# A decoder step on one core: gate chain moved between query chunks, attention values and last sums regrouped, unused products ahead of waits

## The chip, the core and the metric

The kernel runs on one core of a Trainium2 chip. The metric is device microseconds of one launch. A core has TensorE (PE; PEld is its weight load), VectorE (DVE), ScalarE (ACT), GpSimd (POOL) and a queue engine (SP) that issues most DMAs. The engines run their own instruction streams and meet only at semaphores.

## The reference

One step of a trunk with two layers over 512 prompt tokens and 8 x 4 sample tokens (544 rows of 1024). Layer 0 is retention beside memory attention, layer 1 is forgetting attention beside memory attention. Each ends in an output projection, a layer norm, a two-level router that gives every token two of 32 experts, the experts, and a second layer norm.

```python
h = x @ w_in_a; r, s = retention(q, k, v, s0, log_gamma); tok = head_norm(r) * silu(g)     # layer 0
kvf = x @ w_kv_shared; logf = log_sigmoid(f_logit + b_forget); c = cumsum(logf)            # after layer 0
logits = q @ k * scale + c_q - c_k; p = softmax(causal(logits)); tok = p @ v               # layer 1, 12 heads
mem = softmax(mq @ mem_k * scale) @ mem_v                                                  # both layers, 4 heads
x = layer_norm(ALPHA * x + concat(tok, mem) @ w_o); x = layer_norm(ALPHA * x + moe(x))     # both layers
```

## The kernel before, in words

Everything lies in one function `build`, which writes one instruction stream per engine by hand. The order of work on an engine is the order of its text. A `wait_ge` on a semaphore holds all that stands behind it on that engine. Tokens are five tiles of rows (four of 128, one of 32). PSUM has eight banks of 128 x 512, and each stage names its banks.

- **Split products** (`split_product`, lines 706 to 708): projections are done as three products of rounded and remainder parts. Weights come in chunks through two ring buffers: SP loads a chunk (L402) when the chunk two earlier has been used, ACT rounds it (`round_chunk`, L1389), DVE forms the remainder (`split_chunk`, L1823).
- **Gating** (L1134): 30 transposes turn the gated retention rows; PE waits for DVE's scaling (L2156).
- **Memory attention** (`mem_prompt_attention`): for each of four row tiles PE makes logits (L737), DVE takes the maximum (L1763), ACT the exponentials (L1428), DVE scales the rows (L1777), PE turns them (L749), ACT and DVE copy them, PE multiplies by the values (L761). Between these, ACT rounds the eight slices of the output weights (L1400) and DVE forms their remainders. `mem_sample_attention` then turns the cached keys of eight sequences (L783, copied by ACT at L1454), makes their logits (L795), turns the exponentials (L802) and multiplies (L810).
- **Projection and routing** (`project_and_route`, lines 855 to 889): tile by tile PE projects (`project_tile`, two halves of 512 columns), DVE adds the residual (L1860) and normalises (`norm_tile`, lines 1842 to 1850), PE turns the rows (`cols_of`, L700), ACT copies them (`copy_cols`, L1364) and PE makes the router's logits (`router_tile`, L827). Tile i is projected, and directly after it tile i-1 is turned and routed. ACT copies tile i-1 only after it has taken the deviation of tile i (L1369). After the last tile come the slots for experts (L851 to L888) and the gather of the first rows (POOL, L571).
- **Experts** (`experts`, `pair`): 16 pairs; up-products L907, hidden transposes L915, down-products L924. SP streams the weights (L449, L454) as buffers come free. The first pair's buffers are loaded when the last projection is done, the second pair's after the last router tile.
- **Between the layers**: `next_mem_kv` (turning L975, products L1000, both on PE) stands beside `combine(0)` on DVE. Then 20 tiles of keys and values (`token_major`), the 12 gate columns (`gate_columns`, from a chunk of their own), the turning of the keys (L1190), and eight query products (`feature_major`, chunks of `w_in_b`). After the eighth, ACT takes the exponential and the logarithm of the gates (L1662, L1664), and PE makes the running sums (L1207 to L1217).
- **Forgetting attention, prompt**: a pipeline over 12 heads. `minus_c` (L1228) spreads -c over 128 rows by four products; `fox_logits` (L1239); DVE adds and masks (L2199 to L2207); ACT takes the exponentials; `fox_turn` (L1251) makes ten transposes; `fox_values` (L1261) makes ten products with 128 x 128 probabilities as the weights and 64 columns of V moving; DVE scales into `o_rows` (L2213), which 24 transposes turn at the end (L1319).
- **Forgetting attention, samples**: 16 cached pages are turned (L1284) and multiplied (L1307); exponentials L1705; turning L1325; values L1334 and L1339.
- **The end** (`combine(1)`): SP loads the two expert rows of each token two tiles ahead (L497); DVE scales and adds them (L2042, L2043), normalises, and SP stores the tile (L563, L565).

Of the kernel before, what the change touches and what calls it, by code (L numbers as in the profile page):

```python
# [127 lines left out]
def build(nc, x_prompt, x_sample, mem_prompt, state_ret, cache_fox_k, cache_fox_v, cache_fox_logf, cache_mem_k,  # L128
# [12 lines left out]
    with ctx:  # L141
# [98 lines left out]
        eps_ln, eps_hn = sm(1), sm(1)  # L240
        wslot = sm(PAIRS + MORE)
# [25 lines left out]
        chunks.append((cols(w_kv_shared, 1536, 1548), ("tm_mm", 41)))  # L267
# [3 lines left out]
        CH_A, CH_S, CH_B, CH_END = 0, 9, 14, 17  # L271
# [5 lines left out]
        def w_lo(m):  # L277
            return w_raw(m, ring_r)
# [33 lines left out]
        yg = [view(work, 0, 2, D), view(big, 0, 2, D)]  # L312
        RB = 0
# [43 lines left out]
        gate_cols = view(work, 3072, TOK)  # L357

# [4 lines left out]
        PT_AT = {3: 0, 2: 4 * P, 0: 7 * P, 1: 8 * P}  # L363
        LOGIT_AT = {1: (0, 0), 0: (1, 0), 2: (1, P), 3: (2, 0)}
        o_rows = view(x_cols_t, 0, ST, FW)
# [12 lines left out]
        own_row = view(ln_t, (PG * DB + 1) * QR, DB, QR)  # L378
        fkT = [view(work, 3072, 6, P), view(work, 3840, 6, P)]
# [11 lines left out]
        def _(sp):  # L391
# [98 lines left out]
            def expert_rows(l, i):  # L490
                if i == 0:
                    sp.wait_ge(S("y_out"), 16 * PAIRS * (l + 1))
                    sp.wait_ge(S("rows_done"), l + 1)
                if i >= 2:
                    sp.wait_ge(S("yg_used"), NT * l + i - 1)
                n = ROWS[i]
                sp.dma_start(yg[i % 2][0:n], ys.rearrange("(j t) d -> t j d", j=2)[P * i:P * i + n]) \  # L497
                    .then_inc(S(f"yg_in{i % 2}"), 16)
# [58 lines left out]
            for i in range(2):  # L557
                expert_rows(1, i)
            for i in range(2, NT):
                expert_rows(1, i)  # L560
# [8 lines left out]
        def _(pool):  # L569
# [8 lines left out]
            def dispatch(l):  # L578
# [4 lines left out]
                nc.gpsimd.memset(xg, 0.0).then_inc(S("xg_zero"), 1)  # L583
                pool.wait_ge(S("slots"), 3 * l + 1)
                pool.wait_ge(S("xs_out"), 80 * (l + 1))
                pool.wait_ge(S("xg_zero"), l + 1)
# [29 lines left out]
            def mem_outputs(l):  # L616
                pool.wait_ge(S("mkv_ev"), (4, 6)[l])
                for out, lo in ((mem_k_p, 0), (mem_v_p, MW)):
                    pool.dma_start(out[l, 0].rearrange("(t p) h d -> p t (h d)", p=P), memkv[:, l, :, lo:lo + MW]) \
                        .then_inc(S("mp_out"), 16)  # L620
# [24 lines left out]
            pool.dma_start(fox_f_p[0].rearrange("(t p) h -> p t h", p=P), logf[:, 0:ST]).then_inc(S("f_out"), 16)  # L645
            pool.dma_start(fox_f_s.rearrange("b t h -> (b t) h"), logf[0:NS, ST]).then_inc(S("f_out"), 16)
# [5 lines left out]
            pool.wait_ge(S("pool_zero"), 2)  # L652
# [22 lines left out]
            pool.wait_ge(S("f_out"), 32)  # L675
            pool.wait_ge(S("kv_out"), 64)
            pool.wait_ge(S("mp_out"), 64)
# [6 lines left out]
        def _(pe):  # L684
            mm, tr = nc.tensor.matmul, nc.tensor.transpose

# [40 lines left out]
            def mem_prompt_attention(l):  # L727
# [13 lines left out]
                def turn(i):  # L741
                    pe.wait_ge(S("mp_n"), n0 + i + 1)
# [30 lines left out]
            def mem_sample_attention(l):  # L773
# [24 lines left out]
                pe.wait_ge(S("ms_e"), l + 1)  # L798
# [4 lines left out]
                last.then_inc(S("ms_t"), 1)  # L803
                pe.wait_ge(S("ms_c"), l + 1)
# [8 lines left out]
                last.then_inc(S("ms_o"), 1)  # L813

            def mem_sample_columns(l):
                pe.wait_ge(S("ms_n"), l + 1)
                for g in range(2):
                    last = tr(bank(2, P * g, P * g + P), mres[:, g].rearrange("p r d -> p (r d)"), ident)
                last.then_inc(S("ms_r"), 1)
# [11 lines left out]
            def project_tile(l, i):  # L831
# [3 lines left out]
                for half in range(2):  # L835
# [19 lines left out]
            def project_and_route(l):  # L855
# [7 lines left out]
                for i in range(NT + 1):  # L863
                    if 1 <= i < NT:
                        project_tile(l, i)
                    if i == NT - 1:
                        pe.wait_ge(S("onehot"), 2 * l + 1)
                        ranks = rank_bank(l)
                        mm(ranks[:, 0:3], C("strict"), cnt[:, 0:3], start=True, stop=False)
                        mm(ranks[:, 1:3], C("ones"), cnt[:, 0:2], start=False, stop=False)  # L870
                        mm(ranks[:, 2:3], C("ones"), cnt[:, 0:1], start=False, stop=True).then_inc(S("rank_mm"), 1)
# [57 lines left out]
            def experts(l):  # L929
# [4 lines left out]
                pe.wait_ge(S("slots"), 3 * l + 1)  # L934
                pe.wait_ge(S("xg_in"), 16 * (s + 1))
# [57 lines left out]
            def next_mem_kv():  # L993
                pe.wait_ge(S("mem_in"), 64)
# [131 lines left out]
            pe.wait_ge(S("rkd"), 2 * ST + RH)  # L1126
            for i in range(NT):
# [19 lines left out]
            def gate_columns():  # L1147

                chunk_split(pe, 13)
                pe.wait_ge(S("tm_ev"), 38)  # L1150
                w_hi, w_rest = w_r(13), w_lo(13)
                for o, t in ((bank(4, FM0, rows=(0, FH)), slice(0, TOK // 2)),
                             (bank(5, 0, TOK // 2, rows=(0, FH)), slice(TOK // 2, TOK))):
                    for k in range(KD):
                        last = split_product(o, w_hi[:, k, :], w_rest[:, k, :], XT_r[:, k, t], XT_lo[:, k, t], k)
# [37 lines left out]
            pe.wait_ge(S("tk_cp"), NT + NT)  # L1193
            for n in range(2, 10):
                m = CH_B + (n - 2) // 3
                if (n - 2) % 3 == 0:
                    chunk_split(pe, m)
# [4 lines left out]
            pe.wait_ge(S("f_step"), 5)  # L1202
            pe.wait_ge(S("tm_ev"), 42)
            pe.wait_ge(S("pf_in"), 16 * DB * PG)
            for i in range(ST):
                for q in range(i + 1):
# [1076 lines left out]
```

## Time and profile before

| | |
|---|---|
| runs | 1586.42, 1588.14, 1590.35 us, median 1588.14 |
| profiled execution | 1593.53 us, its span 1591.6 us |
| busy | PE 1294.4 us, PEld 890.6, DVE 505.0, ACT 357.4, POOL 101.3 |
| DMA | 316.29 MB, mean 199 GB/s, 420 GB/s in the expert stages |
| mean granted TensorE clock | 0.892 |
| stages, from the chain of waits | layer 0 to the experts 0 to 448 us, experts 448 to 703, keys and queries to 926, prompt heads to 1021, sample pages to 1111, memory and projection to 1284, experts to 1535, end |

The page gives each engine's busy share in 40 equal slices, the TensorE clock that was granted in each (1.00 is 2.4 GHz, 0.50 is 1.2 GHz), and the chain of work that ended last. PE matmul records of float32 products come in twos, so a count of records is twice the count of products there.

### The profile page before, as it was taken

To read this page: it belongs to the slowest core of one execution; us is meant where nothing else is said; L and a number is where in the kernel's file an instruction comes from. 1 tells how busy PE (TensorE), PEld (TensorE's weight loads), DVE (VectorE), ACT (ScalarE), POOL (GpSimd) and SP (SyncE) were. 2 spreads that over 40 slices of the span, in tenths; PEclk is the share of its full clock that TensorE was granted. 3 is DMA by queue.
4 is the path that set the end of the run, shared out by engine and by line. 5 is a ranking of instruction groups with operands and counts; after the bars stand their busy time and mean duration, and the time that the engine had idled before them with its cause. 6 is when DMAs were issued, how large, how long until landed. Compare 5 with 4: busy or idle time off the path is not lost.

```text
span 1591.6 us, 17891 instructions
## 1 busy us (share of the span) xinstructions
PE 1294.4 (81%) x7095; PEld 890.6 (56%) x7095; DVE 505.0 (32%) x1059; ACT 357.4 (22%) x721; POOL 101.3 (6%) x131
## 2 busy tenths in 40 slices
PE   7999987598798777668897899998598799877750
PEld 6999985466543232235796878783466543232220
DVE  3551176533620000008301057314534620000017
ACT  3112232420111111113212236311520111111110
POOL 0000001000011111102000020000000011111100
PEclk9999998797789999988898969798797789999985
DMA  7222117300589999955114140131600589999953
GB/s 284 93 80 80 54 50 237 97 14 27 212 360 420 421 419 420 420 211 203 40 42 164 44 144 1 32 125 46 201 14 27 206 358 420 420 419 420 420 193 111
DMA packets 101991, 316.29 MB, mean 199 GB/s; under 512 B 23058, under 2 KB 55970, under 8 KB 77090
## 3 DMA queue, kind: packets, MB, share of 16 engines
q1 hardware_dynamic: 88978, 284.98, 46.4%
q0 software_dynamic: 12944, 30.36, 5.1%
q8 instruction: 47, 0.77, 0.2%
q14 instruction: 22, 0.18, 0.0%
HBM read 299.61 MB, written 31.42 MB: 208 GB/s over the span
## 4 chain that ended last, share of the span: by engine, by line
PE 58%; DMA 25%; DVE 10%; ACT 4%; issue 1%; SPq 1%; ACTq 0%; POOLq 0%; DVEq 0%
DMA weight_ring<-in_w_up_dram 16%; PE ps L706 9%; PE ps L708 9%; PE ps L707 9%; PE ps L907 6%; DMA mix_cols<-in_w_down_dram 5%; PE ps L924 3%; PE ps L1239 2%; PE ps L1261 2%; PE ps L827 2%; PE ps L1307 2%; DVE small L1842 1%; PE ps L795 1%; DMA work<-stream_rows,ints 1%; PE ps L1000 1%
## 5 line engine op out<-in xcount | busy, mean ns | idle before, releaser
L907 PE MATMUL ps<-expert_weights,work 128*64 128x512 f32 x512 | 128.7, 651 | 39.5 <-DMA expert_weights<-in_w_up_dram 37.0
L2019 DVE TENSOR_TENSOR work<-ps,work 128x256 f32<-128x256 f32 x32 | 13.6, 425 | 439.4 <-ACT work L1494 439.4
L907 PE MATMUL ps<-weight_ring,work 128*64 128x512 f32 x512 | 119.3, 611 | 36.3 <-DMA weight_ring<-in_w_up_dram 36.3
L907 PEld LDWEIGHTS ps<-expert_weights,work 128*64 128x64 f32 x512 | 39.4, 148 | 126.7 <-issue 73.3
L707 PE MATMUL ps<-weight_ring_r,mix_cols_r 128*128 128x384 f32 (+1 forms) x320 | 110.1, 344 | 0.0
L708 PE MATMUL ps<-mix_cols_r,weight_ring_r 128*128 128x272 f32 (+1 forms) x368 | 106.1, 288 | 0.0
L907 PEld LDWEIGHTS ps<-weight_ring,work 128*64 128x64 f32 x512 | 39.7, 139 | 114.9 <-issue 80.5
L1494 ACT ACTIVATE work<-ps 128x256 f32<-128x256 f32 x32 | 12.3, 383 | 277.7 <-PE ps L907 277.7
L924 PE MATMUL ps<-mix_cols,work 128*64 128x512 f32 x256 | 60.2, 611 | 11.5 <-DVE work L2021 6.7
L706 PE MATMUL ps<-expert_weights_r 128*128 128x512 f32 (+1 forms) x160 | 69.1, 432 | 0.0
L708 PEld LDWEIGHTS ps<-mix_cols_r,weight_ring_r 128*128 128x128 f32 (+1 forms) x368 | 67.8, 184 | 0.5
L1504 ACT ACTIVATE work<-ps,small 128x512 f32<-128x512 f32 x64 | 40.5, 683 | 122.7 <-PE ps L924 119.1
L707 PE MATMUL ps<-weight_ring_r,expert_weights_r 128*128 128x512 f32 (+1 forms) x160 | 67.8, 424 | 0.0
L708 PE MATMUL ps<-expert_weights_r,mix_cols_r 128*128 128x512 f32 (+1 forms) x160 | 67.4, 421 | 0.0
L924 PE MATMUL ps<-expert_weights,work 128*64 128x512 f32 x256 | 58.5, 597 | 10.5 <-DVE work L2021 7.9
L706 PE MATMUL ps<-weight_ring_r,mix_cols_r 128*128 128x384 f32 (+1 forms) x160 | 56.7, 354 | 6.1 <-DVE x_cols_r L1815 5.2
L707 PEld LDWEIGHTS ps<-weight_ring_r,mix_cols_r 128*128 128x128 f32 (+1 forms) x320 | 56.6, 177 | 4.3
L706 PE MATMUL ps<-mix_cols_r,weight_ring_r 128*128 128x272 f32 (+1 forms) x192 | 55.7, 290 | 1.6 <-DVE weight_ring_r L1823 1.6
L708 PE MATMUL ps<-weight_ring_r,x_cols_r 128*128 128x384 f32 (+1 forms) x160 | 56.1, 351 | 0.0
L707 PE MATMUL ps<-x_cols_r,weight_ring_r 128*128 128x272 f32 (+1 forms) x192 | 55.2, 288 | 0.0
L1823 DVE TENSOR_TENSOR weight_ring_r<-weight_ring,weight_ring_r 128x1536 fp32r<-128x1536 f32 (+2 forms) x18 | 26.7, 1523 | 83.7 <-ACT weight_ring_r L1389 83.7
L706 PE MATMUL ps<-mix_cols_r,work_r 128*128 128x272 f32 x176 | 51.1, 290 | 0.2 <-ACT expert_weights L1650 0.2
(403 smaller groups left out, 2373.7 us busy)
## 6 DMA issues: line engine op xcount, KB each, us to landing
expert_weights<-in_w_up_dram SPq DMA_DIRECT2D x64, 1024.0 KB, 19.6
weight_ring<-in_w_up_dram SPq DMA_DIRECT2D x64, 1024.0 KB, 20.1
expert_weights<-in_w_down_dram SPq DMA_DIRECT2D x32, 1024.0 KB, 21.9
mix_cols<-in_w_down_dram SPq DMA_DIRECT2D x32, 1024.0 KB, 23.1
weight_ring<-in_w_in_a_dram SPq DMA_DIRECT2D x8, 1536.0 KB, 6.5
weight_ring<-in_w_o_dram SPq DMA_DIRECT2D x4, 2048.0 KB, 13.3
weight_ring<-in_w_kv_shared_dram SPq DMA_DIRECT2D x4, 1536.0 KB, 8.0
weight_ring<-in_cache_fox_k_dram SPq DMA_DIRECT2D x12, 384.0 KB, 4.4
```

The source lines that it names most:

```text
L706: mm(o, a_r, b_r, start=(k == 0), stop=False)
L707: mm(o, a_r, b_lo, start=False, stop=False)
L708: return mm(o, a_lo, b_r, start=False, stop=(k == KD - 1))
L795: last = mm(bank(b // 4, 0, ML, rows=rr), qmb[:, a, 16 * b:16 * b + 32], mkcT[:, b % 2, a, :], start=(a == 0), stop=(a == 1), skip_group_c ...
L827: last = mm(bank(2 + j % 2, 0, NG + NE, rows=(0, n)), XT[:, k, P * i:P * i + n], wr[:, k, :], start=(k == 0), stop=(k == KD - 1))
L907: last = mm(bank(0, rows=(t.start, t.stop)), xgT[:, k, t], WU[2 * q + j][:, k, :], start=(k == 0), stop=(k == KD - 1))
L924: last = mm(bank(4 + half, rows=(t.start, t.stop)), hid_cols[:, f, t], WD[2 * q + j][:, f, 512 * half:512 * half + 512], start=(f == 0), s ...
L1239: last = mm(bank(b, o, o + P * (i + 1)), qT[f, h // 2, P * i:P * i + P], kT[f, h // 2, 0:P * (i + 1)], start=True, stop=True)
L1261: last = mm(bank(7, FD * i, FD * i + FD), fprT[:, h % 2, o:o + P], V[:, q, FD * h:FD * h + FD], start=(q == 0), stop=(q == i))
L1307: last = mm(o, qbd[:, h, b, :], fkT[n % 2][:, h, :], start=False, stop=False, skip_group_check=True)
L1504: last = af(yb[:, 512 * half:512 * half + 512], bank(4 + half), ACT.Copy, scale=wslot[:, i:i + 1])
L1823: v.tensor_tensor(w_lo(m)[:, k, :], w_raw(m)[:, k, :], w_r(m)[:, k, :], ALU.subtract) \
```

## The change

Parts, lettered as the prediction names them. **Unused products**: `keep_clock(b, n)` issues n products of 128 x 512 into a bank that nobody reads; it stands ahead of waits in six places. **Router order**: `project_tile` takes halves, and the router of tile i-2 stands between the halves of tile i; the rank products move behind the last projection. **Gates**: the 12 gate columns leave the chunk ring and get a load of their own; the query chunks therefore come one place earlier. The gate chain on ACT and DVE stands between query chunks and the running sums before query product 8. **Heads**: -c is turned once (`turn_c`) and spread by one product a head; values go by pairs of heads with V as weights, already turned; the reciprocals of the sums are taken once and spread by `row_sums`. **Banks** of the sample stage move from 4-7 to 0-3 and back. **End**: all five row tiles are loaded at once, PE adds the two rows, DVE adds that to the stream, ACT takes sums and squares. Several semaphores are merged under one name.

```diff
+            def keep_clock(b, n):
+                lo = CONST["decay"][0]
+                for _ in range(n):
+                    mm(bank(b), ident, const_t[:, lo:lo + 512], start=True, stop=True)
...
                 def turn(i):
+                    keep_clock(7, 3)
                     pe.wait_ge(S("mp_n"), n0 + i + 1)
...
+                    if b == 0:
+                        keep_clock(7, 4)
                     pe.wait_ge(S("mk_cp"), n0 + b + 1)
...
-                pe.wait_ge(S("ms_e"), l + 1)
+                keep_clock(7, 2)
+                pe.wait_ge(S("ms_step"), 8 * l + 2)
...
                 pe.wait_ge(S("slots"), 3 * l + 1)
+                keep_clock(1, 3)
                 pe.wait_ge(S("xg_in"), 16 * (s + 1))
...
             def next_mem_kv():
+                keep_clock(1, 5)
                 pe.wait_ge(S("mem_in"), 64)
...
+            keep_clock(0, 6)
             for i in range(NT):
                 n = ROWS[i]
                 pe.wait_ge(S("gated"), i + 1)
...
-                for i in range(NT + 1):
-                    if 1 <= i < NT:
-                        project_tile(l, i)
-                    if i == NT - 1:
-                        pe.wait_ge(S("onehot"), 2 * l + 1)
-                        ranks = rank_bank(l)
...
-                    if i:
-                        cols_of(2 * l + 1, i - 1)
-                        router_tile(l, i - 1)
+                project_tile(l, 1)
+                cols_of(2 * l + 1, 0)
+                for i in range(2, NT):
+                    project_tile(l, i, (0,))
+                    router_tile(l, i - 2)
+                    project_tile(l, i, (1,))
+                    cols_of(2 * l + 1, i - 1)
+                pe.wait_ge(S("onehot"), 2 * l + 1)
+                ranks = rank_bank(l)
...
+                router_tile(l, NT - 2)
+                cols_of(2 * l + 1, NT - 1)
+                router_tile(l, NT - 1)
...
-        chunks.append((cols(w_kv_shared, 1536, 1548), ("tm_mm", 41)))
...
+            sp.wait_ge(S("mt_mm"), 8)
+            sp.dma_start(gate_w, cols(w_kv_shared, 1536, 1548)).then_inc(S("gate_w"), 16)
...
+                if j == 34:
+                    act.wait_ge(S("gate_w"), 16)
+                    af(gate_r, gate_w, ACT.Copy).then_inc(S("gate_w"), 1)
-                if j in (22, 26, 31, 36):
+                if j in (22, 26, 31, 37):
                     round_chunk(CH_S + 1 + (j - 20) // 5)
...
-            round_chunk(CH_B)
...
             for n in range(2, 10):
                 m = CH_B + (n - 2) // 3
+                if n == 8:
+                    gate_sums()
...
+                if n == 3:
+                    act.wait_ge(S("f_step"), 1)
+                    af(fe, fe, ACT.Exp, scale=-1.0).then_inc(S("f_step"), 1)
+                if n == 4:
+                    act.wait_ge(S("f_step"), 3)
+                    af(fe, fe, ACT.Ln).then_inc(S("f_step"), 1)
...
-                for q in range(ST):
-                    last = mm(bank(3, P * q, P * q + P), negc[:, q, h:h + 1].broadcast_to([P, P]), ident,
-                              start=True, stop=True)
-                last.then_inc(S("fnb"), 1)
+                mm(bank(3), ident[0:FH, h:h + 1].broadcast_to([FH, P]), negc_cols[0:FH], start=True, stop=True) \
+                    .then_inc(S("fnb"), 1)
...
+                for q in range(ST):
+                    i0 = max(q, 1)
+                    for r in range(2):
+                        rows = (64 * r, 64 * r + 64)
+                        v_q = V[:, q, FD * (2 * p + r):FD * (2 * p + r) + FD]
+                        if q == ST - 1:
+                            moving = fprT[:, r, 9 * P:10 * P]
+                        else:
+                            moving = fprT[:, r, 0:9 * P].rearrange("p (i t) -> p i t", i=3)[:, i0 - 1:, P * q:P * q + P]
+                        last = mm(bank(7, P * i0, SEQ, rows=rows), v_q, moving, start=(q == 0), stop=(q == ST - 1),
+                                  skip_group_check=True)
...
+            for p in range(FH // 2):
+                row_sums(p)
...
+            for i in range(NT):
+                n = ROWS[i]
+                pe.wait_ge(S(f"yl_in{i}"), 16)
+                for half in range(2):
+                    b = 2 * (i % 2) + half
+                    if i >= 2:
+                        pe.wait_ge(S("yg_ev"), 2 * (i - 2) + half + 1)
+                    for j in range(2):
+                        last = mm(bank(b, rows=(0, n)), ident[0:n, 0:n], yg1[i][0:n, j, 512 * half:512 * half + 512],
+                                  start=(j == 0), stop=(j == 1))
+                    last.then_inc(S("yg_sum"), 1)
...
+            def sums_and_deviation(i):
+                n = ROWS[i]
+                act.wait_ge(S("yg_ev"), 2 * i + 2)
+                af(squares[0:n], X[0:n, i], ACT.Copy, accum_out=row_sum[0:n, i:i + 1]).then_inc(S("ln_sq"), 1)
...
+                af(squares[0:n], X[0:n, i], ACT.Square, bias=less_mean[0:n, i:i + 1],
+                   accum_out=row_sq[0:n, i:i + 1]).then_inc(S("ln_sq"), 1)
...
+                af(rstd[0:n, i:i + 1], row_sq[0:n, i:i + 1], ACT.Sqrt, bias=eps_ln[0:n, 0:1], scale=1.0 / D) \
+                    .then_inc(S("ln_sd"), 1)
```

## Rows read from the trace of the kernel before

**Rows 1.** The page: the span, and the granted clock in 40 slices.
```profile
span 1591.6 us, 17891 instructions
...
PEclk9999998797789999988898969798797789999985
```

**Rows 2.** The chain of waits, experts of layer 0: start us, us, what.
```profile
447.61 9.22 PE ps L907 x32
...
475.11 6.87 PE ps L907 x32
...
496.31 28.23 DMA weight_ring<-in_w_up_dram
```

**Rows 3.** What PE waited for, whole span: us in total, times, longest us.
```profile
PE ps L827 <- ACT x_cols L1364: 25.7, 10, 4.5
PE ps L749 <- DVE work L1777: 23.4, 8, 4.1
...
PE ps L1134 <- DVE work L2156: 6.5, 1, 6.5
```

**Rows 4.** Busy by stretch: us, PE, PEld, DVE, ACT, POOL, clock, DMA share, GB/s.
```profile
281.00:306.00 25.00, 16.05 (x96) 12.90 (x96) 9.63 (x15) 9.28 (x28) 0.00 (x0) 0.66 0.46 116
313.00:333.00 20.00, 17.26 (x88) 8.27 (x92) 4.85 (x8) 7.54 (x14) 0.00 (x0) 0.77 0.00 1
...
944.00:1007.00 63.00, 63.00 (x439) 52.13 (x437) 48.55 (x115) 38.41 (x111) 0.00 (x0) 1.00 0.00 1
1008.00:1029.00 21.00, 19.09 (x93) 17.05 (x94) 1.78 (x5) 4.61 (x13) 0.00 (x0) 0.51 0.12 38
1029.00:1082.00 53.00, 50.42 (x448) 41.11 (x445) 7.48 (x16) 12.87 (x25) 0.00 (x0) 1.00 0.40 125
```

**Rows 5.** The chain of waits, queries and prompt heads.
```profile
841.93 12.73 DMA weight_ring<-in_w_in_b_dram
...
926.37 4.56 PE ps L1239 x8
...
947.61 2.35 PE ps L1239 x8
...
951.20 2.18 PE ps L1261 x20
...
957.92 2.18 PE ps L1261 x20
```

**Rows 6.** PE in order of time: start us, us, what, wait and releaser; memory attention.
```profile
281.56 1.97 PE L749 MATMUL ps<-const,work 128*128 128x128 f32 x8 [4.10 <-DVE work L1777]
...
313.01 1.91 PE L795 MATMUL ps<-work,mem_queries 128*32 128x256 f32 x4 [4.20 <-ACT work L1454]
...
333.38 0.50 PE L706 MATMUL ps<-expert_weights_r 128*128 128x512 f32 x1
```

**Rows 7.** DVE in order of time: the residual's last half, first and last tile.
```profile
344.81 0.69 DVE L1860 SCALAR_TENSOR_TENSOR x_rows<-x_rows,ps 128x512 f32<-128x512 f32 x1 [4.88 <-PE ps L708]
...
417.24 0.68 DVE L1860 SCALAR_TENSOR_TENSOR x_rows<-x_rows,ps 32x512 f32<-32x512 f32 x1 [4.81 <-PE ps L708]
```

**Rows 8.** PE in order of time, turning and routing of one tile.
```profile
398.74 1.04 PE L700 MATMUL ps<-const,x_rows 128*128 128x128 f32 x8
402.54 2.19 PE L827 MATMUL ps<-weight_ring,x_cols 128*128 128x36 f32 x16 [2.77 <-ACT x_cols L1364]
```

**Rows 9.** PE in order of time, keys' turning and gate sums.
```profile
858.38 3.45 PE L1190 MATMUL ps<-const,work 128*128 128x128 f32 x18 [9.19 <-ACT expert_weights L1650]
...
915.39 4.45 PE L1207 MATMUL ps<-small,const 128*128 128x12 f32 x20 [4.62 <-DVE small L2179]
```

**Rows 10.** All engines in order of time, the end.
```profile
1547.05 1.23 DVE L2042 SCALAR_TENSOR_TENSOR x_rows<-x_rows,work 128x1024 f32<-128x1024 f32 x1 [7.52 <-DMA work<-expert_rows]
...
1581.08 0.34 SPq L565 DMA_DIRECT2D out_dram<-x_rows  x1
```

**Rows 11.** Groups by line: ACT's table loads ahead of the square roots.
```profile
L1369 ACT ACT_TABLE_LOAD x4 | 5.1, 1283 | 4.8 <-DMA expert_rows<-work,ints 4.7
```

More of the change, by code:

```diff
@@ L312, in build @@
         yg = [view(work, 0, 2, D), view(big, 0, 2, D)]
+        yg1 = [view(big, 2 * D * i, 2, D) for i in range(NT)]
+        squares = view(work, 0, D)
         RB = 0
@@ L357, in build @@
         gate_cols = view(work, 3072, TOK)
+        gate_w, gate_lo = view(work, 3616, KD, FH), view(work_r, 3616, KD, FH)
+        gate_r = view(work_r, 3712, KD, FH)
         fpr = [view(work, 4 * SEQ * k, ST, SEQ) for k in range(2)]
@@ L829, in router_tile, with project_tile @@
                 last.then_inc(S("rt_mm"), 1)
-            def project_tile(l, i):
+            def project_tile(l, i, halves=(0, 1)):
                 n = ROWS[i]
                 pe.wait_ge(S("mix_lo"), NT * l + i + 1)
-                for half in range(2):
+                for half in halves:
                     j = 10 * l + 2 * i + half
@@ L1268, in _, with row_sums @@
                     fox_logits(s)
+                if s % 2 and s >= 3:
+                    fox_values(s // 2 - 1)
                 if 1 <= s <= FH:
                     fox_turn(s - 1)
-                if s >= 2:
-                    fox_values(s - 2)
                 if s + 1 < FH:
                     minus_c(s + 1)
-            pe.wait_ge(S("fp_ev"), FH)
+            pe.wait_ge(S("fp_ev"), FH // 2)
+            pe.wait_ge(S("fp_r"), 1)
+            for i in range(ST):
+                last = tr(bank(3, P * i, P * i + P, rows=(0, FH)), esum_f[:, i, :], ident)
+            last.then_inc(S("fp_r"), 1)
+            def row_sums(p):
+                if p >= 4:
+                    pe.wait_ge(S("tk_cp"), 2 * NT + p - 3)
+                for r in range(2):
+                    last = mm(bank(4 + p % 4, rows=(64 * r, 64 * r + 64)),
+                              ident[0:FH, 2 * p + r:2 * p + r + 1].broadcast_to([FH, FD]), rsum_cols[0:FH], start=True,
+                              stop=True)
+                last.then_inc(S("tk_mm"), 1)
             def turn_page(n):
@@ L1673, in _ @@
             act.wait_ge(S("kv_out"), 64)
+            act.wait_ge(S("fnb"), 1)
+            af(negc_cols[0:FH], bank(7, rows=(0, FH)), ACT.Copy).then_inc(S("fnb_cp"), 1)
             keys_sum(0)
@@ L1686, in _ @@
                     if n == 0 and h >= 2:
-                        act.wait_ge(S("fox_p"), h - 1)
-                    w = 4 * P if n < 2 else 2 * P
-                    af(fprT[:, h % 2, 4 * P * n:4 * P * n + w], bank(4 + n, 0, w), ACT.Copy).then_inc(S("fp_c"), 1)
+                        act.wait_ge(S("fox_p"), h // 2)
+                    lo, hi = PC_AT[n]
+                    af(fprT[:, h % 2, lo:hi], bank(4 + n, 0, hi - lo), ACT.Copy).then_inc(S("fp_c"), 1)
                 if h + 2 < FH:
                     keys_sum(h + 2)
+            act.wait_ge(S("fp_r"), 2)
+            af(rsum_cols[0:FH], bank(3, rows=(0, FH)), ACT.Copy).then_inc(S("fp_r"), 1)
             for n in range(DB * PG):
@@ L1727, in _ @@
             experts(1)
-            norm_and_columns(3, columns=False)
+            for i in range(NT):
+                sums_and_deviation(i)
         @block.vector
```

270 lines of the change are left out of this document (144 added, 126 removed).

## The prediction

> **What bounds the kernel now.** I read the page first [rows 1]: the chain of work that ended last is PE's in most stages, the experts apart, and the granted clock has gaps outside them. The chain of waits then gives the stages: from 496 us on, the experts of layer 0 wait for one load of weights after another [rows 2]. Those loads are released by the first pair's products and by the last projections, so whatever comes earlier ahead of them moves the whole stage earlier, one for one. The list of PE's waits names three that the change aims at: the router for its copied columns 25.7 us, the turning of memory probabilities 23.4, the gating 6.5 [rows 3]. The busy time by stretch shows what such waits cost besides their length: in the memory attention the clock is 0.66 and 0.77, at the end of the heads 0.51, and in the run of heads and of pages 1.00 [rows 4]. The same eight logit products take 4.56 us where the clock is 0.50 and 2.35 where it is 1.00, 1.94 times [rows 5]. So the gain can come from three things: shorter idle time, PE's own work at the higher level (2.4 in place of 1.2 GHz), and less work.
>
> **One unused product.** The up-products of a pair are 32 records of 512 columns, two side by side in 64-wide halves: 6.87 us at full clock, 0.43 a record, and 9.22 while the clock is coming back [rows 2]. A float32 product leaves two records, so one unused product is 0.86 us at full clock and 0.86 x 1.94 = 1.66 at half. Three stand in front of a wait of 23.4/8 = 2.9 on average [rows 3]: 2.6 fit at full clock, 5.0 at half do not. Four stand in front of the first keys' copy, 3.4 against 4.20 [rows 6]; six before the gating, 5.1 against 6.5 [rows 3]. At full clock all of them hide; at half clock they push the stage out.
>
> **The sum**, in us of the profiled execution, each term with its two ends:
>
> Gating: the transposes behind the wait run at the higher level, but DVE's scaling paces most of them: -2 (0 to -3).
>
> Memory attention, prompt, each layer: 16.05 us of PE work at a clock of 0.66 would be 16.05 x 0.66 = 10.6 at 1.00, so -5.5 if the waits between stay [rows 4]. Next to end last would be ACT's rounding of the output weights, done between the same steps. Ends 0 and -9. Samples: 17.26 x (1 - 0.77) = -4.0 (0 to -6). Two layers: -11 and -8.
>
> Router order, each layer. From the first projection at 333.4 [rows 6] the residual of tile 0 starts at 344.8 and that of tile 4 at 417.2 [rows 7]. A tile's projection is 11.2 us (333.4 to 344.6, the tile of 32 rows too, since 512 columns move in every one). Turning takes 1.04 and routing 2.19, and between them PE waits 2.77 for ACT [rows 8]. In the new order the router of tile i-2 has half a projection, 5.6 us, between its turning and itself, twice the wait. PE then does 5 x 11.2 + 3 x 2.2 + 3 x 1.05 + 0.2 = 66, and the last projection ends at 399.4 where it ended at 417.2 less 0.8. I take -17 (the choice of experts on DVE now stands before the last residual; ends -10 and -18), twice: -34. The experts' loads wait for that projection and move with it.
>
> Products before the gather and before the next memory rows: three and five, 5.0 and 8.3 us if they start at half clock. Against that, the first pair's products would go from 9.22 towards 6.87 [rows 2], twice, and DVE's combining covers the second. I take 0 for all of it (-6 to +8).
>
> Keys and queries. Today the chunk of query weights is loaded last (12.73 us on the chain, landing at 854.7 [rows 5]) and the keys' turning waits 9.19 for its rounding [rows 9]. One chunk fewer in the ring puts it a place earlier: -9.6. After the queries PE waits 4.62 for the gate chain on ACT and DVE, then does the sums, of which the first group is 4.45 at half clock [rows 9]; the first logits start at 926.4 [rows 5], 15.6 us behind the last query product (915.39 - 4.62 = 910.8). The chain now runs beside queries 3 to 6, the sums cost 4.1 at full clock ahead of query 8, and about 2.8 are left for turning and spreading -c: -9. Together -18.6 (-12 to -20).
>
> Heads. One head's period is 957.92 - 951.20 = 6.72, of which the values are 2.18 [rows 5]. Two heads' values are now 2,560 columns in two halves at 0.43 per 512, that is 2.15 for both: a pair takes 13.45 - 2.2 = 11.25, six pairs -13.2. The clock before the loop no longer falls, so the first two heads lose their doubled products (2.2 for the logits of each, about 1 for each spreading): -6. Together -19 (-10 to -23). DVE comes next: 48.55 busy of 63 [rows 4], 5.2 a head of which about 0.4 goes, under PE's 5.6.
>
> Sample pages: 24 transposes and their copies become six spreads, and the stretch at 0.51 [rows 4] would be shorter by up to half of its 19.1: -6 (-2 to -9).
>
> The end. Five tiles take DVE 6.8 each, 1547.05 to 1581.08 [rows 10]. New: two adds of 0.69 [rows 7] and two passes of 1.23 [rows 10] with small ones, 4.2; ACT takes two passes, by DVE's row about 3.3 with its small ones. That is -13, but the first tile has to go through PE (four products, 3.4 or 6.6) and ACT, which is some 8 late: -5. If PE stays at half clock, 5 x 6.6 = 33 alone ends it: -9 to +8.
>
> Sum: -2 - 11 - 8 - 34 + 0 - 18.6 - 19 - 6 - 5 = -103.6. The profiled execution took 1593.5, 5.4 above the median, so the change is set against the median: 1588.1 - 103.6 = **1484.5**.
>
> **A rule against the sum.** Long runs made of turns and products together hold 1.00 here (1029 to 1082 [rows 4]). The Trainium skill ("TensorE: Matmul & The Clock Gate", Part 4: PE-mode transpose) says that the full clock does not engage for transposes, as they do not count as busy work in the same way. By it the two memory terms, mostly turns, would give half, and the sum would be about -94; the row stands against it.
>
> **The rivals.** First, the order does less than it says: ACT's copies stay late, so that a layer's router wins only 10, and DVE's chain of maximum and mask holds the heads at 6.72. For it: DVE's 48.55 of 63. Against it: 2.77 of wait against 5.6 of cover. 14 and 13 are lost: 1484.5 + 27 = 1511.5.
>
> Second, the unused products run at half clock and overrun: eight times 5.0 - 2.9, twice 6.6 - 4.2, the gating 3.5, the two ahead of the sample's turning and those before the gather some 6, about 31 in all; and the 21 of gating and memory attention do not come: 1536. For it: the clock is 0.66 where the first of them stand [rows 4]. Against it: they are themselves work without gaps.
>
> Third, Square is not in the table set that Sqrt needs: two loads of 1.283 [rows 11] a tile bring ACT to 5.9 against DVE's 4.2, 10 in all: 1494.5. The Trainium skill ("ScalarE: Activation LUTs", "Table sets: the hidden batching unit") names relu, copy, identity and abs as in every set, and not Square, so it leaves this open; no row shows it.
>
> Fourth, the other side: PE's clock does not hold in the new heads and pages. Heads that are paired let PE pause in every second step, and at half clock the loop's 67.5 become 131 and the pages' 50.4 become 98 [rows 4]: +111, which gives 1595, slower by 7. It decides if the whole stretch from 905 on is at 0.50. For it: 19.09 of 21 us busy at 0.51. Against it: 1.00 from 944 to 1007, and fewer pauses ahead of the loop.
>
> **How the numbers follow.** Forecast 0.57, first rival 0.20, second 0.08, third 0.10, fourth 0.05. 0.3%, about what a measurement can tell from no change, is 4.8 us. Only the fourth, full in force (0.03), is slower; a milder one (0.01) lies within; all else is faster, 0.96. Low end: all the better ends of the terms together are 25 lower, 1460. High end: the first rival with 10 on top, 1522; left out are the second, the fourth and some of the tails.
>
> **What would show it.** Right: PE's wait at the router is gone and the last projection ends 17 earlier; the clock in the memory attention is over 0.9; no wait for the query chunk before the keys; a head every 5.6 us; the last stage 28 us long with a tile each 4.2. Wrong: unused products that still run when their wait has ended, a clock near 0.5 in the heads, table loads beside the square roots of the end, or DVE's idle time gone in the heads with a period over 6.

## The result, and the profile after

| | before | after |
|---|---|---|
| median of the runs | 1587.28 us | 1503.74 us |
| lowest, highest | 1583.45, 1590.35 | 1501.96, 1505.48 |
| profiled execution, its span | 1593.53, 1591.6 | 1503.13, 1501.2 |
| mean granted clock | 0.892 | 0.933 |

The changed kernel is faster: ratio 0.9475, interval 0.945 to 0.9499, that is 83.5 us. The forecast was 1484.5, with a range of 1460 to 1522. The two profiled executions lie 90.4 apart; that of before was itself about 6 above its median.

The page of the kernel after, to be read against [rows 1]:

```profile
span 1501.2 us, 17781 instructions
...
PEclk9999998999799999998899968999999699999987
```

Three slices of the clock stand out now: the one where the experts' slots are made (the 11th), one near 880 us (the 24th, a 6), and the second slot stage (the 32nd). The one near 880 is where the heads begin; the kernel before has a 6 in the same place, so this stretch got nothing back.

What PE waited for, in us in total, times and the longest:

```profile
PE ps L1405 <- DMA expert_weights<-expert_rows: 7.1, 1, 7.1
...
PE ps L844 <- ACT x_cols L1419: 5.8, 4, 2.5
...
PE ps L763 <- DVE work L1847: 1.8, 2, 1.3
```

The router's wait went from 25.7 to 5.8 and the memory turning's from 23.4 to 1.8 [rows 3]; the gating's 6.5 has left the list. L1405 is new: PE adds the rows of the end.

Busy time by stretch (PE, PEld, DVE, ACT, POOL, then clock, DMA share, GB/s), first the memory attention, then the heads' start and run:

```profile
278.00:301.00 23.00, 20.58 (x120) 11.74 (x120) 12.83 (x21) 12.65 (x42) 0.00 (x0) 1.00 0.68 196
301.00:322.00 21.00, 19.36 (x96) 9.64 (x96) 10.02 (x11) 12.09 (x21) 0.00 (x0) 1.00 0.01 1
...
878.00:910.00 32.00, 32.00 (x76) 15.59 (x76) 18.91 (x40) 13.24 (x35) 6.62 (x17) 0.53 0.56 195
910.00:955.00 45.00, 45.00 (x232) 25.44 (x230) 36.01 (x78) 32.64 (x93) 0.00 (x0) 0.99 0.00 1
```

The memory attention runs at 1.00 where it had 0.66 and 0.77 [rows 4]. In the heads PE is busy for all of 878 to 910 and has half its clock.

The chain of waits, from the first spread of -c on (L1252 spread, L1262 logits, L1274 turning, L1294 values):

```profile
877.50 1.09 PE ps L1252 x2
878.59 3.53 PE ps L1262 x8
882.12 2.00 PE ps L1252 x2
884.11 4.56 PE ps L1262 x8
888.67 2.32 PE ps L1274 x10
891.00 2.00 PE ps L1252 x2
893.00 4.56 PE ps L1262 x8
...
907.08 3.62 PE ps L1294 x16
910.70 1.24 PE ps L1274 x10
911.94 1.05 PE ps L1252 x2
912.99 2.35 PE ps L1262 x8
```

The same eight records of logits take 4.56 until 906 and 2.35 from 913 on. PE had been idle for 1.34 us ahead of 877.5; the clock fell 2 us behind that, with PE busy.

Setting the two chains side by side gives what each part moved (start of the same work, before and after; the last column is the change since the line above):

| up to the start of | before | after | moved | this part |
|---|---|---|---|---|
| last retention products | 258.5 | 257.2 | -1.3 | no part of the change |
| first memory exponentials (gating) | 278.1 | 278.6 | +0.5 | +1.8 |
| first projection (memory attention) | 333.4 | 324.5 | -8.9 | -9.4 |
| second slot products (router order) | 432.8 | 403.8 | -29.0 | -20.1 |
| fourth pair of experts | 487.7 | 459.3 | -28.4 | +0.6 |
| first chunk of keys | 761.7 | 729.9 | -31.8 | -3.4 |
| first logits (gates, queries) | 926.4 | 878.6 | -47.8 | -16.0 |
| first page turned (heads) | 1021.1 | 968.0 | -53.1 | -5.3 |
| last values of the pages | 1102.0 | 1044.3 | -57.7 | -4.6 |
| slot products of layer 1 (memory, router) | 1269.1 | 1182.5 | -86.6 | -28.9 |
| first rows of the end | 1547.0 | 1462.0 | -85.0 | +1.6 |
| last store | 1581.1 | 1490.7 | -90.3 | -5.3 |

One line is far from its forecast: the heads, -5.3 for -19. The gain of the router order shows in the chain as full speed: routing a tile takes 1.71 (2.19 in [rows 8]), turning one 0.87, and by the two chains the last residual starts 63.8 us behind the first projection, where it started 83.8 behind it.

```profile
353.68 1.71 PE ps L844 x16
...
388.30 1.28 DVE x_rows L1930 x2
```

### The profile page after: what moved, and what is told of

Same layout as the page of the kernel before. It is cut to its first block, busy times and chain, and to the rows that moved or that the text cites. A ratio compares the mean times of both kernels' runs of the same rounds, so it can differ in the third digit from the quotient of the medians.

```text
span 1501.2 us, 17781 instructions
## 1 busy us (share of the span) xinstructions
PE 1308.6 (87%) x7057; PEld 851.5 (57%) x7057; DVE 492.9 (33%) x1032; ACT 369.0 (25%) x743; POOL 102.0 (7%) x131
## 4 chain that ended last, share of the span: by engine, by line
PE 59%; DMA 25%; DVE 10%; ACT 4%; issue 1%; SPq 1%; POOLq 0%; DVEq 0%; ACTq 0%
DMA weight_ring<-in_w_up_dram 16%; PE ps L719 9%; PE ps L721 9%; PE ps L720 9%; PE ps L927 6%; DMA mix_cols<-in_w_down_dram 6%; PE ps L944 3%; PE ps L1262 2%; PE ps L698 2%; PE ps L1356 2%; PE ps L1252 1%; PE ps L811 1%; PE ps L1274 1%; PE ps L1294 1%; PE ps L1333 1%
## 5 line engine op out<-in xcount | busy, mean ns | idle before, releaser
L927 PE MATMUL ps<-expert_weights,work 128*64 128x512 f32 x512 | 124.4, 633 | 38.3 <-DMA expert_weights<-in_w_up_dram 35.6
L927 PE MATMUL ps<-weight_ring,work 128*64 128x512 f32 x512 | 122.7, 625 | 34.9 <-DMA weight_ring<-in_w_up_dram 34.9
L721 PE MATMUL ps<-mix_cols_r,weight_ring_r 128*128 128x272 f32 x352 | 102.4, 291 | 0.0
L944 PE MATMUL ps<-mix_cols,work 128*64 128x512 f32 x256 | 60.2, 611 | 11.1 <-DVE work L2091 7.3
L944 PE MATMUL ps<-expert_weights,work 128*64 128x512 f32 x256 | 58.5, 597 | 11.3 <-DVE work L2091 6.7
L721 PEld LDWEIGHTS ps<-mix_cols_r,weight_ring_r 128*128 128x128 f32 x352 | 67.2, 191 | 0.0
L719 PE MATMUL ps<-expert_weights_r 128*128 128x512 f32 (+1 forms) x160 | 64.1, 401 | 0.9 <-DVE mix_cols_r L1904 0.9
L719 PE MATMUL ps<-mix_cols_r,weight_ring_r 128*128 128x272 f32 x208 | 61.5, 296 | 1.8 <-DVE weight_ring_r L1893 1.7
L720 PE MATMUL ps<-weight_ring_r,expert_weights_r 128*128 128x512 f32 (+1 forms) x160 | 63.1, 394 | 0.0
L721 PE MATMUL ps<-expert_weights_r,mix_cols_r 128*128 128x512 f32 (+1 forms) x160 | 63.0, 394 | 0.0
L720 PE MATMUL ps<-x_cols_r,weight_ring_r 128*128 128x272 f32 x208 | 60.8, 292 | 0.0
L698 PE MATMUL ps<-const 128*128 128x512 f32 x106 | 58.4, 697 | 1.0 <-DVE ints L2096 1.0
L1893 DVE TENSOR_TENSOR weight_ring_r<-weight_ring,weight_ring_r 128x1536 fp32r<-128x1536 f32 (+1 forms) x18 | 28.7, 1637 | 74.5 <-ACT weight_ring_r L1444 74.5
```

The lines of the kernel that those rows point to most:

```text
L698: mm(bank(b), ident, const_t[:, lo:lo + 512], start=True, stop=True)
L719: mm(o, a_r, b_r, start=(k == 0), stop=False)
L720: mm(o, a_r, b_lo, start=False, stop=False)
L721: return mm(o, a_lo, b_r, start=False, stop=(k == KD - 1))
L927: last = mm(bank(0, rows=(t.start, t.stop)), xgT[:, k, t], WU[2 * q + j][:, k, :], start=(k == 0), stop=(k == KD - 1))
L944: last = mm(bank(4 + half, rows=(t.start, t.stop)), hid_cols[:, f, t], WD[2 * q + j][:, f, 512 * half:512 * half + 512], start=(f == 0), s ...
```

## The experiments

Medians of four runs (six for the last three kernels), each beside runs of the kernel before on the same chip. The chips differ between groups of runs, and the medians of the kernel before lie between 1584.4 and 1590.9 there, so a difference of a few us between two groups tells nothing. Every edit is against the changed kernel unless another is named. The line numbers of these kernels are a few higher than those above.

### A spread of -c over all rows

```diff
-                mm(bank(3), ident[0:FH, h:h + 1].broadcast_to([FH, P]), negc_cols[0:FH], start=True, stop=True)
+                mm(bank(3), ident[:, h:h + 1].broadcast_to([P, P]), negc_cols, start=True, stop=True)
...
+            nc.gpsimd.memset(negc_cols, 0.0).then_inc(S("pool_zero"), 1)
```

> The changed kernel with -c spread by 128 rows of contraction (116 of them zero) in place of 12; the number of columns stays 512 a head. Theory (the heads' missing gain is a clock that stays at 0.50 from 879 to 910 us because the stretch from the last query to the first values is done by thin products, 12-row spreads and 64-row logits): with full rows the clock comes back behind the first turn, as it did in the kernel before, near 892 instead of 910; three steps at half clock become about one and a half, 8 to 12 us are won, about 1493. Rival (the pause of 1.3 us ahead of the first spread lets the clock fall and only time or dense work brings it back, the spread's rows are no matter): unchanged, 1502 to 1506, clock back near 910.

Measured: 1490.99 (ratio 0.9381, 0.9325 to 0.9437), 12.8 below the changed kernel, and 13.2 below the kernel with the pause filled, two sections on, which ran on the same chip. The spread moves as many columns as before. Busy time by stretch of this kernel:

```profile
882.00:886.00 4.00, 4.00 (x12) 1.59 (x11) 3.90 (x8) 1.88 (x2) 3.38 (x12) 1.00 0.99 323
886.00:890.00 4.00, 2.66 (x12) 1.98 (x12) 3.90 (x11) 3.48 (x11) 1.33 (x3) 0.80 1.00 341
890.00:894.00 4.00, 4.00 (x11) 1.56 (x10) 2.11 (x6) 2.74 (x9) 0.00 (x0) 0.77 0.97 342
894.00:898.00 4.00, 4.00 (x20) 2.52 (x20) 3.90 (x10) 2.71 (x7) 0.00 (x0) 1.00 0.96 347
```

The first logits run at full clock, and the dip, behind a wait of 1.3 us, is some 4 us long (0.61 and 0.54 between 888 and 892). The number came out near the theory's 1493. Not all of it is clock. In the run of the loop, where both kernels have 1.00, the spread of 128 rows takes 0.86 in the chain and the one of 12 rows 1.05, so that a pair of heads takes 11.22 (902.85 to 914.07) in place of 11.60 (912.99 to 924.59):

```profile
902.85 2.35 PE ps L1264 x8
...
906.45 0.86 PE ps L1254 x2
```

Twelve times 0.19 is about 2 of the 12.8; why the thin spread takes longer is not shown.

### The zeroing alone

The control: POOL's zeroing and ACT's wait for it stay, the spread has 12 rows again.

> The changed kernel with what the wide spread needed (the columns of -c zeroed by POOL, ACT's copy waiting for that) and the 12-row spread left as it is. Theory (the rows of the spread hold the clock, not the zeroing or a shifted start): as the changed kernel, 1501 to 1507, clock at 0.50 for 15 to 30 us at the start of the heads. Rival (the wide spread won by a shift in time): as the wide spread, 1490 to 1493.

Measured: 1503.13 (0.9456, 0.9408 to 0.9504), as the changed kernel. In its chain of waits the doubled logits are back:

```profile
876.61 3.57 PE ps L1264 x8
...
882.17 4.56 PE ps L1264 x8
...
899.95 4.56 PE ps L1264 x8
...
911.01 2.35 PE ps L1264 x8
```

So it is the rows of the spread, and not a shift in time, that won 12 us.

### The pause filled

```diff
             turn_c()
+            keep_clock(6, 2)
             pe.wait_ge(S("fm_ev"), 10)
```

> The changed kernel with two unused products behind the turning of -c, in the 1.34 us that PE waits ahead of the first spread. Theory (thin products): the clock still falls near 880 and still comes back near 910; 1503 to 1505. Rival (the pause): the clock holds 1.00 into the heads, the first three steps take 4.6, 4.6 and 4.6 in place of 5.5 and 8.9 each, 13 us won, about 1490.

Measured: 1504.22 (0.9474, 0.9417 to 0.9531). The time is the theory's, and PE has no gap. The clock falls all the same, but not as the theory had it: it comes back at 895, falls again twice, and the sum is as before:

```profile
882.00:886.00 4.00, 4.00 (x13) 2.19 (x11) 3.74 (x10) 3.22 (x11) 1.26 (x3) 0.50 1.00 372
...
894.00:898.00 4.00, 4.00 (x15) 2.14 (x13) 3.03 (x9) 3.24 (x9) 0.00 (x0) 0.92 0.13 49
898.00:902.00 4.00, 4.00 (x21) 1.91 (x20) 3.62 (x8) 0.74 (x4) 0.00 (x0) 0.57 0.00 0
```

Later, logits of 4.56 stand at 922.7 in this run's chain. So the pause is not what brings the clock down. With the 12-row spread it can fall later in the loop too, though it need not: the changed kernel held 0.99 from 910 to 955.

### Unused products in the first steps

```diff
                 if s + 1 < FH:
                     minus_c(s + 1)
+                if s < 3:
+                    keep_clock(7, 3)
```

> The changed kernel with three unused products of 128 rows behind each of the first three steps of the head loop (nine, 7.7 us at full clock, 15 at half). Theory (thin products): the dense products bring the clock back within the first step; steps 1 and 2 go from 8.9 to 4.6 plus 2.6, the third as well, so that 3 to 6 us are won net, 1498 to 1501, and the clock is 1.00 from about 892 on. Rival (the clock comes back only some 30 us after its fall, whatever runs): it comes back near 910 all the same, and 15 us are added, about 1518.

Measured: 1508.51, 1498.9 to 1512.0 (0.9474, 0.9409 to 0.9539). The median is a miss for both. The profiled execution is the slowest of the four: its clock is back by 892, as the theory said, but logits at half clock stand again at 920.1 (4.56), so what the nine products won was paid once more. The fastest of the four, 1498.9, has a mean clock of 0.945 where this one has 0.933 and lies within the theory's range. In the trace that there is, products put in one place did not help the places behind it; that they never do is not shown.

### No unused products

All six places are left out.

> The changed kernel without any of its unused products. Theory (my sum): the memory attention gives back 6 and 3.4 in each layer, 19 together; gating and the gathers, where the products overran (8.0 at half clock where 6.5 had been waited), give 2 and twice 2.5 the other way, next to nothing for the memory rows: about +12 on the changed kernel, 1516, with the clock of the memory stage back at 0.66 to 0.77. Rival (the waits in the memory attention set its length and its clock is of no matter): 1496 to 1500, faster than the changed kernel.

Measured: 1521.55 (0.9578, 0.9517 to 0.964), 17.8 above the changed kernel. The memory stage, from the first exponentials to the first projection, is 54.5 (280.85 to 335.33) in place of 45.9, so two layers make 17.2 of it, and its clock is down to 0.67 and 0.74:

```profile
278.00:305.00 27.00, 15.17 (x88) 11.29 (x88) 12.52 (x19) 12.11 (x40) 0.00 (x0) 0.67 0.63 188
305.00:330.00 25.00, 20.59 (x104) 12.48 (x104) 10.54 (x11) 12.46 (x19) 0.00 (x0) 0.74 0.00 0
```

The theory's size for that part held (8.6 a layer for 9.4), while its deductions did not show: by the total, the products at the gating and the gathers do not cost the 7 that it took off.

### The products of the memory attention alone

On the wide-spread kernel, without `keep_clock(0, 6)`, `(1, 3)` and `(1, 5)`.

> The wide-spread kernel with the unused products of the memory attention alone; those before the gating, the gathers and the next memory rows are left out. Theory (these overran at half clock and only gave back what they cost): within 3 of the wide-spread kernel, 1488 to 1494, the first pair of experts starting 2.7 earlier and the fourth about 1 earlier. Rival (they keep the clock for what comes behind them and earn their place): 1495 to 1500.

Measured: 1493.70, 1487.9 to 1499.5 (0.9395, 0.934 to 0.9449), within the theory's 3. The up-products of the first pairs, chain of waits, in the wide-spread kernel

```profile
423.53 7.09 PE ps L929 x32
...
436.33 6.87 PE ps L929 x32
...
461.47 6.88 PE ps L929 x32
```

and without those products

```profile
421.10 10.10 PE ps L929 x32
...
436.91 6.87 PE ps L929 x32
...
462.05 6.88 PE ps L929 x32
```

The first pair starts 2.4 earlier and takes 3 longer; by the second pair nothing is left, and the fourth starts 0.6 later. The 0 that the prediction took for these products is what they are worth, as far as runs that spread over 12 us can tell.

### The old router order

> The changed kernel with the router order of the kernel before (tile i-1 turned and routed behind tile i, rank products ahead of the last turnings). Theory (the order is worth 20 a layer, as the traces have it): the wait at the router is back, 2.6 a tile, and the time is 1503.7 + 40 = 1544 (1538 to 1548). Rival (the clock that the memory attention keeps up would have shortened the old order as well): half of that, about 1524.

The edit puts the loop of before back into `project_and_route`, nothing else. Measured: 1543.78, 1538.5 to 1546.4 (0.9699, 0.9649 to 0.9749), 40.0 above the changed kernel, the theory's number. PE's waits in this run have the row of [rows 3] again, word for word but for the line numbers:

```profile
PE ps L844 <- ACT x_cols L1416: 25.7, 10, 4.5
```

### Products ahead of the end

On the wide-spread kernel, `keep_clock(7, 4)` in front of the wait for the first rows of the end.

> The wide-spread kernel with four unused products (6.6 us at half clock) in the 7.1 us that PE waits for the first rows of the end. Theory: the first tile's products then run at full clock, 3.4 in place of 6.0, and the end is 2 to 3 shorter: 1488. Rival (the products or the wait behind them overrun, or the clock is not back by then): 1491 to 1493.

Measured: 1490.26 (0.9381, 0.9328 to 0.9434), 0.7 below the wide spread, less than the runs can tell. The trace has the theory's step: the first tile's eight records take 3.71 (5.74 with the wide spread alone), and from the rows' landing to the last store it is 26.4 us where it was 28.4.

```profile
1445.67 5.40 PE L700 MATMUL ps<-const 128*128 128x512 f32 x8 [0.96 <-DVE ints L2100]
1452.98 17.55 PE L1408 MATMUL ps<-expert_weights,const 128*128 128x512 f32 x40 [1.91 <-DMA expert_weights<-expert_rows]
```

### A spread over 64 rows

On the wide-spread kernel, `ident[0:64, ...]` and `negc_cols[0:64]`.

> The wide-spread kernel with 64 rows of contraction in the spread in place of 128 (the upper half left out; the values are the same). Theory (what counts is how much of the array the stretch uses): between the two, the clock falls at the start of the heads for longer than with 128 rows and shorter than with 12: 1494 to 1500. Rival (a spread of more than a few rows is enough, or the clock looks at time busy alone): as with 128 rows, 1489 to 1493.

Measured: 1490.04 (0.9378, 0.9332 to 0.9424), the rival's number, but not the rival's reason. At the start the clock is where the theory put it, lower than with 128 rows: 0.50 from 888 to 900. What pays for it is the run of the loop (PE in order of time):

```profile
909.11 0.69 PE L1254 MATMUL ps<-ln_gb,const 64*128 64x512 f32 x1
909.11 0.70 PE L1264 MATMUL ps<-expert_weights 64*128 64x256 f32 x2
909.64 0.59 PE L1254 MATMUL ps<-ln_gb,const 64*128 64x512 f32 x1
909.65 1.89 PE L1264 MATMUL ps<-expert_weights 64*128 64x128 f32 x6
```

Spread and logits start together. The odd heads' logits use the upper 64 rows and the spread the lower, so the two run side by side: both are done after 2.43, where the logits alone take 2.42. A pair of heads takes 10.36 (905.78 to 916.14) in place of 11.22. A time that agrees with a theory does not yet show it.

### Towards the best kernel

First, on the kernel with products ahead of the end: the six spreads of the reciprocals over 128 rows, and a small exponential on ACT between the queries, which loads the table early.

> The kernel with the wide spread and the four products ahead of the end, with the six spreads of the reciprocals over 128 rows as well and the exponential's table loaded between the queries (1.28 us ahead of the first head's exponentials). Theory: the sample stage behind the spreads runs at full clock earlier, its first values 1.9 in place of 3.7, and the table load leaves the heads' start: 2 to 4 less than the kernel with products at the end, 1486 to 1488. Rival (the spreads of the reciprocals are too few to hold the clock, and the table is hidden): 1489 to 1491.

Measured: 1485.82 (0.9345, 0.9308 to 0.9381). The spreads take 5.2, the first values behind them 1.86 as all the others (6.7 and 3.2 in the kernel that it builds on), and the table load stands at 852.5 beside the queries. What each of the two edits is worth was not measured apart.

Second, on that one, the spread over 64 rows, in the half that the head's logits leave free:

```diff
+                o = 64 * ((h + 1) % 2)
+                mm(bank(3), ident[o:o + 64, o + h:o + h + 1].broadcast_to([64, P]), negc_cols[o:o + 64], start=True, stop=True)
...
+            af(negc_cols[64:64 + FH], bank(7, rows=(0, FH)), ACT.Copy).then_inc(S("fnb_cp"), 1)
```

> The best kernel so far with the spread over 64 rows, for each head the half of the array that its logits don't use. The trace of the 64-row kernel shows the spread and the logits of the odd heads starting together, so that an odd head's logits and spread take 2.05 less 1.1 and a pair 10.36 in place of 11.22. Theory (this holds for even heads as well): a pair takes 9.3 to 9.5 at full clock unless DVE (5.0 a head) bounds it, then 10.0; over five pairs 6 are won, and 4 to 6 given back by the clock, which falls for longer with 64 rows at the start of the heads: 1482 to 1486. Rival (DVE's chain or ACT's copies bound the pair at 10.4 already): 1486 to 1490.

Measured: 1481.39, 1475.3 to 1484.5 (0.9309, 0.9274 to 0.9345). A pair takes 10.26 (892.01 to 902.27). Now PE waits for ACT's exponentials in each second step:

```profile
901.41 0.93 PE L1277 MATMUL ps<-const,work 128*128 128x128 f32 x6 [0.33 <-ACT work L1763]
```

So a pair is only 0.1 shorter than with the spread in the lower half for all heads, and close to the 10.0 that the theory gave for a loop bound by DVE; that the chain of maximum, exponentials and turning sets it is read from these waits and not tested.

Third, three unused products ahead of the first turning.

> As the kernel with halves, and three unused products in front of the first head's turning, where PE waits some 2 us for the exponentials. Theory: they fill the wait and the clock is back before the second head, 3 to 6 less than without them. Rival (as in the run with nine products, they run at half clock and cost what they win): the same within 2.

Measured: 1476.39, 1474.0 to 1483.7 (0.9291, 0.9256 to 0.9325), 5.0 below the one without, though the ranges of the two overlap and the two profiled executions lie 2.1 apart. The clock is 1.00 from 884 on, where the other has 0.65 until 888 and 0.93 until 892. By its median this is the fastest kernel of the study, 27 below the changed one.

## Why the prediction was right, point by point

**What held.** The three waits went, and their prices were those of the sum. Router order: 20.1 a layer by the chain and 40.0 for two layers by the run that undoes it, against 17 a layer. The sum already had the projections at full clock. The surplus is some 2 us in three routers and three turnings, 1.71 and 0.87 each where the sum took 2.2 and 1.05, and 0.8 that the sum took off the end of the old projection, though the last residual starts as soon as that projection ends [rows 7]. Memory attention: 9.4 and 9 against 9.5. Queries and gates: 16.0 against 18.6. What is missing there is clock again. Behind the running sums the last query product runs at half clock, though PE had no gap from 850 on; twenty records at 0.23 in place of 0.13 and the last of the sums make, by estimate, the 2.6:

```profile
861.00:866.00 5.00, 5.00 (x24) 5.00 (x24) 0.79 (x5) 0.00 (x0) 0.00 (x0) 0.50 0.02 3
```

Pages: 4.6 for 6. End: 5.3 for 5; a tile takes 3.9 where 4.2 was said.

**What failed: the term of the heads.** "The clock before the loop no longer falls, so the first two heads lose their doubled products": it fell, near 879.6, with PE busy, and stayed at 0.50 until 910. Steps 0 to 3 took 5.5, 8.9, 8.9 and 11.1, 34.4 together, where by the rows of the same loop at full clock they take 19.7; that is 14.7. A pair in the run of the loop took 11.60 where the sum had 11.25, about 2 in all, because the 12-row spread takes 1.05; the loop's end gave, by difference, some 3 back, and the term missed by 13.7. The step that failed is that I took the change to remove the fall because it removes the wait in front. It also puts a 12-row product in place of four products of 128 rows in each head, and I counted that product's columns and not its rows. The wide spread wins 12.8 back, the control and the filled pause win nothing. Why a spread of 12 rows lets the clock go is not shown by these runs, only that it does.

**The gating** was to win 2 and lost 1.8, but the loss lies ahead of it. The last retention products took 6.2 at a falling clock, behind a wait of 1.50 us for the state's load, where the kernel before took 3.8 behind a wait of 0.42. PE in order of time, first the kernel before, then the changed one:

```profile
258.51 1.94 PE L1106 MATMUL ps<-mix_cols,x_cols 128*32 128x128 f32 x16 [0.42 <-DMA mix_cols<-in_state_ret_dram]
260.37 1.98 PE L1111 MATMUL ps<-x_cols,expert_weights 32*128 32x512 f32 x4
...
257.20 2.52 PE L1128 MATMUL ps<-mix_cols,x_cols 128*32 128x128 f32 x16 [1.50 <-DMA mix_cols<-in_state_ret_dram]
259.65 3.78 PE L1133 MATMUL ps<-x_cols,expert_weights 32*128 32x512 f32 x4
263.36 8.02 PE L698 MATMUL ps<-const 128*128 128x512 f32 x12
```

From their end to the first exponentials it is 15.2 us in place of 15.7. So the gating itself won half a us of its 2: its six products ran mostly at half clock, 8.0 us for the 5.1 of the sum. The run without any products has the same: a wait of 2.15, retention products of 7.3, then 15.9. Why the state's load ends at another time in each run stays open.

**The rest of the miss.** The forecast took the sum off the median of before, though the profiled execution that the sum was read from was some 6 above the median. The two profiles are 90.4 apart, the medians 83.5. So of 19.2 missed, 13.7 are the heads and about 6 this; the others cancel: the gating and the queries came 6 short, and the routers won 6 more than was said. That the time lies well inside the range owes something to this surplus, which was not foreseen. Which stretch of the profiled execution was long was not looked for. Two sums of the prediction are off without bearing on the result: the better ends of its terms are together 32 lower and not 25, so the low end should have been 1452, and the third rival's 1.7 a tile is 8.5 and not 10.

**The rivals.** The first gave 1511.5 and came nearer in time than the forecast, for a reason that did not happen: the router won 40 and not 20, and DVE did not bound the heads (36.0 of 45 busy). The second, products that overrun in the memory attention, did not come: L698 shows 2.84 for six records there, 0.47 a record, the clock of full speed, and the wait behind is 1.8 in all. The third did not come either: the end has a single table load (L1485, 1.28 us, ahead of the first square root), and Square ran without one. The Trainium skill ("ScalarE: Activation LUTs", "Table sets: the hidden batching unit") leaves Square out of the functions that it names for every set; this trace shows it running between square roots with no load. The fourth had the right effect at a small part of its size, half clock for 31 us of the loop and not for all of it, and another cause: it put it down to pauses, and PE had none from 878 to 910. A clock near 0.5 in the heads was also among the prediction's own signs of being wrong.

**The rule on transposes.** The turns of the memory attention, mixed with unused products, ran at 1.00 from 278 to 322, and the two layers won 18.4 of the 19 in the sum. By the Trainium skill's rule ("TensorE: Matmul & The Clock Gate", Part 4: PE-mode transpose) they were to win half of it, so that the rule was the worse guide here. Without the products the same stretch had 0.67, so no run here shows turns holding full clock by themselves.

## What to carry to other kernels

When a product is made thinner, its columns and its rows both have to be asked for: here 12 rows in place of 128 cost 13 us, most of it clock, and ate most of a rewrite's gain. Unused products paid in front of waits that recur within a stage (17 us of 1500 here); at the gating, the gathers and the next memory rows, single waits ahead of dense work, no gain could be told. A product of 64 rows can be put beside another one that uses the other 64, which is worth looking for before any filling.

## What the runs showed of the hardware that was not expected

The granted clock was 0.50 for some 30 us in which PE was busy without a gap (880 to 910); with the same columns and 128 rows in the spread it was below 1.00 for some 4 us only, with 64 rows at 0.50 for 12 (888 to 900). It was also 0.50 from 861 to 866, behind the running sums, with no gap in front. Two products of 64 rows in opposite halves of the array start within 0.01 us of each other and both end in about the time of one. The Trainium skill ("TensorEngine Tiling (Array Packing)", Overview) says that for a contraction of 64 or less the array can be split into independent tiles, for up to twice the speed; the trace agrees that two such products share it, with 0.86 us a pair won for the odd heads alone.
